# Constant matmuls at four seams of a two-block layer kernel

## The reference

```
# first layer
hn     = rmsnorm(x) * norm_g                       # seam "x" is here
proj   = hn @ w_in                                 # 2048 x 12292
ya, yb, yc = three attentions of 4 heads (forgetting, chunked relpos, stick breaking)
merged = sum_n sigmoid(gates_n) * ((y_n * silu(g_n)) @ w_up_n)
x1     = x + merged @ w_out                        # seam "merged" is before this product
# second layer: GLA and mLSTM heads, both directions, context of 256 tokens first
ctx scan inputs = (rmsnorm(ctx) * (1+sc) + sh) @ w_in_2
lat scan inputs = (rmsnorm(x1)  * (1+sc) + sh) @ w_in_2
y      = concat(norm(gla) * silu(..), sigmoid(..) * norm(mlstm))
x2     = x1 + gt1 * (y @ w_out_2)                  # seam "y" is before this product
h2     = rmsnorm(x2) * (1+sc2) + sh2               # seam "x2" is here
out    = rmsnorm(x2 + gt2 * ((silu(conv3x3(h2 @ w_up_gate)) * (h2 @ w_up_val)) @ w_down))
```

## Time and profile before

| | |
|---|---|
| time, median of 3 runs | 2298.99 us (2298.82 to 2306.23) |
| time of the profiled execution | 2298.3 us |
| its span, first to last instruction | 2296.6 us |
| PE busy | 2207.8 us (96%) |
| DVE busy | 1547.5 us (67%) |
| ACT busy | 1052.8 us (46%) |
| mean granted TensorE clock | 0.990 |

### The profile page before, as it was taken

How to read it: one execution, slowest core, us unless ns; L and a number is a source line. 1 busy time by engine, 2 the same in 40 slices (tenths; PEclk the granted TensorE clock), 3 DMA queues, 4 the chain that set the end, 5 groups by cost and what they waited for, 6 DMA issues and landing times.

```text
span 2296.6 us, 29599 instructions
## 1 busy us (share of the span) xinstructions
PE 2207.8 (96%) x10304; PEld 1771.3 (77%) x10304; DVE 1547.5 (67%) x2220; ACT 1052.8 (46%) x1317; POOL 50.7 (2%) x99
## 2 busy tenths in 40 slices
PE   7999999999999999999999998989999999999997
PEld 6777778778887777876887776668888888888886
DVE  5455667767676878675665778557777777775554
ACT  4443435544443535446333444345455555554443
POOL 0000000000001000000000000100000000000000
PEclk9999999999999999999999999999999999999999
DMA  7877778878776979774443323555555556566664
GB/s 272 286 248 255 269 239 275 292 241 277 252 270 225 323 267 347 256 275 129 129 128 120 91 84 92 179 184 171 178 190 184 190 176 200 168 199 226 195 192 130
DMA packets 279625, 482.41 MB, mean 210 GB/s; under 512 B 21687, under 2 KB 112905, under 8 KB 277601
## 3 DMA queue, kind: packets, MB, share of 16 engines
q1 hardware_dynamic: 274464, 464.87, 61.4%
q0 software_dynamic: 5056, 16.15, 2.1%
HBM read 474.49 MB, written 6.46 MB: 209 GB/s over the span
## 4 chain that ended last, share of the span: by engine, by line
PE 81%; DVE 8%; ACT 4%; issue 4%; DMA 2%; SPq 0%; ACTq 0%; DVEq 0%; POOL 0%; POOLq 0%
PE gemm_ps L1647 71%; DVE w_lo L971 2%; ACT w_hi L587 2%; DVE msum L1123 1%; PE ps L1676 1%; PE ps L2022 1%; DVE tmpT L1003 1%; PE ps L2074 1%; PE ps L2160 1%; PE ps L2081 1%; DMA w_raw<-in_w_out_dram 1%; DVE sc L1492 1%; DMA mraw<-in_w_mod_dram 0%; PE ps L1718 0%; DMA w_raw<-in_w_in_dram 0%
## 5 line engine op out<-in xcount | busy, mean ns | idle before, releaser
L971 DVE TENSOR_TENSOR w_lo<-w_raw,w_hi 128x1024 fp32r<-128x1024 f32 (+1 forms) x688 | 827.6, 1215 | 488.0 <-ACT w_hi L587 481.5
L1647 PE MATMUL gemm_ps<-w_hi,a_hi 128*128 128x512 f32 (+1 forms) x2304 | 935.1, 406 | 29.7 <-DVE a_lo L1010 14.5
L587 ACT ACTIVATE w_hi<-w_raw 128x1024 fp32r<-128x1024 f32 (+1 forms) x688 | 710.9, 1049 | 456.0 <-PE gemm_ps L1647 351.4
L1647 PE MATMUL gemm_ps<-w_hi,a_lo 128*128 128x512 f32 (+1 forms) x2304 | 900.4, 391 | 0.0
L1647 PE MATMUL gemm_ps<-w_lo,a_hi 128*128 128x512 f32 (+1 forms) x2304 | 898.7, 390 | 0.0
L1647 PEld LDWEIGHTS gemm_ps<-w_hi,a_hi 128*128 128x128 f32 x2304 | 435.7, 189 | 151.7 <-issue 35.6
L1647 PEld LDWEIGHTS gemm_ps<-w_lo,a_hi 128*128 128x128 f32 x2304 | 436.2, 189 | 91.2 <-issue 8.4
L1647 PEld LDWEIGHTS gemm_ps<-w_hi,a_lo 128*128 128x128 f32 x2304 | 435.0, 189 | 92.6
L1552 DVE SCALAR_TENSOR_TENSOR acc<-gp,cw,acc 128x256 f32<-128x256 f32 x344 | 151.5, 481 | 13.8 <-DVE acc L1552 1.4
L1123 DVE SCALAR_TENSOR_TENSOR msum<-mraw,cs,msum 128x1024 f32<-128x1024 f32 x120 | 153.2, 1277 | 0.9 <-DMA mraw<-in_w_mod_dram 0.2
L1647 PE MATMUL gemm_ps<-w_hi,ft_hi 128*128 128x512 f32 x344 | 135.0, 392 | 2.2 <-DVE w_lo L971 2.2
(11 more groups left out here) (375 smaller groups left out, 1532.3 us busy)
## 6 DMA issues: line engine op xcount, KB each, us to landing
w_raw<-in_w_in_dram SPq DMA_DIRECT2D x336, 512.0 KB, 4.5
mraw<-in_w_mod_dram SPq DMA_DIRECT2D x192, 512.0 KB, 6.1
w_raw<-in_w_up_dram SPq DMA_DIRECT2D x336, 256.0 KB, 3.2
w_raw<-in_w_down_dram SPq DMA_DIRECT2D x84, 512.0 KB, 4.2
w_raw<-in_w_out_dram SPq DMA_DIRECT2D x64, 512.0 KB, 4.7
w_raw<-in_w_up_dram SPq DMA_DIRECT2D x24, 512.0 KB, 5.4
x_d<-xres POOLq DMA_DIRECT2D x2, 2048.0 KB, 7.9
x_sb<-in_x_dram SPq DMA_DIRECT2D x2, 1024.0 KB, 5.9
```

Of the source, the lines that this page charges most:

```text
L587: act.activation(w_hi[:, slot, :, 0:n], raw[:, slot, :, 0:n], ACT.Copy).then_inc(hi_done, 1)
L971: dve.tensor_tensor(w_lo[:, slot, :, 0:n], raw[:, slot, :, 0:n], w_hi[:, slot, :, 0:n].bitcast(F32), ALU.subtract).then_inc(lo_done, 1)
L1647: mm = pe.matmul(gemm_ps[:, bank, rt, 0:n], x[:, chunk0 + k, tok], w[:, slot, kk, 0:n], start=(k == 0 and part == 0), stop=(k == chunks - ...
```

## The change

A helper `keep_busy(bank, n)` multiplies the identity with the first 512 columns of `cst`, n times, into the first half of the bank that the next block will begin anew. Nothing reads these values. The calls are in float32. There are 32 of them: at seam x four before the wait for `diag_set` and five behind the first two turns; at merged five before and three behind; at y four behind; at x2 eight before and three behind. Since the helper reads columns beyond the identity, a wait for `const_in` is added ahead of the first four.

```
+            def keep_busy(bank, n):
+                for _ in range(n):
+                    pe.matmul(gemm_ps[:, bank, 0], ident, cst[:, 0:NBLK], start=True, stop=True)
+
             def product(u0, slot0, bank, hi, lo, units, chunk0=0, after=None, chunks=None, n=NBLK,
                         halfway=None, turning=None, turned=None,
-                        turning_next=None):
+                        turning_next=None, busy=(0, 0)):
                 if turning:
                     turned = turning[0]
+                    keep_busy(bank, busy[0])
                     turn(*turning, 0)
                     turn(*turning, 1)
+                    keep_busy(bank, busy[1])
...
             pe.transpose(pC[:, 0:88], vrows[0:88, :], ident[0:88, 0:88]).then_inc(S("n_vecT"), 1)
+            pe.wait_ge(S("const_in"), 16)
+            keep_busy(0, 4)
             pe.wait_ge(S("diag_set"), 1)
...
-                            turning=("x", x_sb, True, 0) if B == 0 else None)
+                            turning=("x", x_sb, True, 0) if B == 0 else None, busy=(0, 5))
...
                 product(U_OUT + BU * c, 0, c % 2, a_hi, a_lo, BU, turning=("merged", merged, False, 0) if c == 0 else None,
-                        after=after, turning_next=("ctx", ctx_sb, False, 0) if c == DC - 1 else None)
+                        busy=(5, 3), after=after, turning_next=("ctx", ctx_sb, False, 0) if c == DC - 1 else None)
...
-                        halfway=(lambda u: half_step(8 * 12 + u)) if c == 0 else None, turning=("y", y, False, KC // 2) if c == 0 else None)
+                        halfway=(lambda u: half_step(8 * 12 + u)) if c == 0 else None, turning=("y", y, False, KC // 2) if c == 0 else None,
+                        busy=(0, 4))
...
-                        turning=("x2", y, False, 0) if isinstance(b, int) and b == 0 else None,
+                        turning=("x2", y, False, 0) if isinstance(b, int) and b == 0 else None, busy=(8, 3),
```

## The result

The changed kernel takes 2315.89 us (median of 7 runs, 2311.49 to 2316.76) against 2300.26 us of the kernel before on the same chips (7 runs, 2297.75 to 2306.71). The medians differ by 15.6 us. The ratio, which goes by all runs and not by the two medians, is 1.0057, about 13 us, with a 95% interval of 1.0044 to 1.0071: 10 to 16 us slower. Forecast were 15.4 us and a time of 2313.7. Effects of the experiments are given by this ratio too.

What follows compares the result with a forecast made beforehand. TensorE, busy for 96% of the span, was taken to bound the kernel. Seams of 9.2 + 2.1 + 1.05 + 3.0 = 15.4 us, added to 2298.3, gave 2313.7 us; range 2306 to 2321.

Steps and rivals of the forecast that it cites:

- Seam x: First block: turns and calls behind the constants' wait move product start from 19.68 to 30.5, less 1.6 clock: +9.2 us.
- Seam merged: Where TensorE awaits merged: calls start behind L1227, product 5.0 us later, less 2.9 from the clock: +2.1 us.
- upper bound of +4.9: At merged: the cost in us if the clock level falls within the calls and stays low for 5.5 us.
- Seam y: Four calls behind the turns end at 1430.6, product formerly started at 1429.52; no clock to win: +1.05 us.
- Seam x2: Eight calls before the turns, three behind; product starts at 1553.0 instead of 1547.95, less 2.0 clock: +3.0 us.
- room of 3.7 us: At x2, time from L2148's end of issue to the rows being ready, against 6.9 us for eight calls.
- Sum: All four seams: 9.2 + 2.1 + 1.05 + 3.0 = 15.4 us slower, giving 2313.7 us.
- Half price: Rival for all calls: each takes 0.43 us instead of 0.86; +4.2 us in all, 2302.5; chance 0.09.
- The constants don't arrive in time: Rival claimed the opposite at x: constants land before 10.5, whole change +6.5 us, 2304.8; chance 0.05.
- hidden filler: Rival at all seams: calls lie in TensorE's waiting time and the clock comes back; 6.5 us faster, 2291.8; chance 0.03.
- the most the seams could win: Product at full clock gives back 1.6 us at x, 2.9 at merged, 0 at y, 2.0 at x2: 6.5 us.

Runs made afterwards that it cites:

- the two half experiments: Kernel before, changed at seam x only: the constants' wait without calls (one execution, 2304.72 us); nine calls on columns of x without that wait (one execution, 2300.17 us).
- the last run: Changed kernel with all 32 calls, the nine of seam x on columns of x, without the constants' wait: 2306.31 us, ratio 1.0030 to the kernel before.

## Why the prediction was right

- **Seam x.** Predicted a product start at 30.5 and +9.2 us; the trace has 30.46 and +9.6. The constants landed a little earlier (first call at 18.60, not 19.4), the eight rows took 6.2 us and not 5.1. The two errors nearly cancel, and that the start came out to 0.1 us is luck. The 0.4 us that are left lie in the first unit: I gave it 2.73 us at full clock, and behind a call it takes 3.15 (30.46 to 33.61), since its first two matmuls start 0.63 us apart; it is 3.16 at merged and 3.14 at x2. The reasoning that the turns stand behind the new wait, and that five more calls outlast a_lo, is shown by the two half experiments: +2.4 and +0.6 to +1.5 alone, +9.6 together.
- **Seam merged.** Predicted +2.1; +2.5. My sum also counted the 0.35 us of slow transposes behind the first unit, which a seam as measured here leaves out; with them the change costs +2.2. The calls stand behind L1227 as read from the wait's number, and three ahead of it with two behind the turns save 5.0 us against five and three. The upper bound of +4.9 for a level that falls within the calls was near what one execution of the version without the wait had, +4.2. The level held in the profiled execution, but it need not have.
- **Seam y.** Predicted +1.05; 0. This is the step that failed. The product does start late: its first six matmuls are done 5.93 us behind the last one ahead of the seam (1440.94 to 1446.87), against 5.00 before (1426.02 to 1431.02), +0.9. But the turn behind the second unit is at 1453.23, 12.29 us behind that matmul, against 12.28 before. The 1.15 us in which the second unit used to wait for its a_lo are now 0.22. The wait before, and the rows after:

```profile
1435.43 0.50 PE L1647 MATMUL gemm_ps<-w_hi,a_hi 128*128 128x512 f32 x1 [1.15 <-DVE a_lo L1010]
...
1442.05 3.60 PE L1627 MATMUL gemm_ps<-cst 128*128 128x512 f32 x8
1445.08 0.79 PE L1654 MATMUL gemm_ps<-w_hi,a_hi 128*128 128x512 f32 x1
...
1450.36 0.50 PE L1654 MATMUL gemm_ps<-w_hi,a_hi 128*128 128x512 f32 x1 [0.22 <-DVE a_lo L1010]
...
1453.23 0.60 PE L1725 MATMUL ps<-cst,xn 128*128 128x128 f32 x4
```

  The two other traces with four calls at y agree (12.27 and 12.30 us). I had looked only at the first wait of this block, and the next one swallowed the delay. The 1.05 us too many here were partly made up by 0.4 us too few at x, which is luck.
- **Seam x2.** Predicted +3.0; +3.0. The room of 3.7 us against eight calls, and the low level at their start, are both in the trace; with three and two calls the seam is 4.6 us shorter.
- **Sum.** Seams 9.6 + 2.5 + 0 + 3.0 = 15.1 us against 15.4 predicted; the runs give 10 to 16, 13 by the ratio. A sum of single seams, one of which (x) moves by itself from 22.59 to 24.96, isn't as exact as a miss of 0.3 us suggests. The total of the profiled execution, +18.1 us, holds 3 us of drift that no seam explains.
- **The rivals.** Half price is out: 64 rows for 32 calls. The constants don't arrive in time; the last run, which does without their wait, shows what it would have been: 4 to 9 us slower, where I had given 6.5. The mechanism of the hidden filler, with chance 0.03, is right wherever calls stand ahead of the wait and fit: a version made so is 5 to 11 us faster than before, around the 6.5 us that I gave as the most the seams could win. That figure counted only product matmuls at the low level. The turns gain too: 8 rows take 1.94 us at x2 before and 1.04 in the changed kernel.

## What to carry to other kernels

Work that shall keep TensorE warm must stand ahead of the wait that it is to cover, and its length must fit that wait; put behind the semaphore that ends the wait, it is paid for with its own time (4.4 us for five calls at merged), less what the clock gives back. An overrun costs nothing only if a later wait of the same engine swallows it, as 0.9 us at y: follow the chain to the next waits, not only to the first. Check what the filler itself has to wait for: a late operand here turned calls worth 0.6 to 1.5 us into 9.6. Price a filler by its rows at both clock levels, and ask what the clock can give back at most (here 6.5 us) before adding 27 us of it.

## What was not expected of the hardware

- At merged the level fell in all five traces without calls there, each with both waits open, 2.62 us ahead of the turns and about 1.7 behind them. With the second one covered and the first left open it held (8.67 us for the seam), in one execution. In two of the five it fell under the turns, before the second wait, and once it fell within calls behind the first wait (15.34 us). When it falls isn't settled by these runs.
- At seam x the same instructions ran at different levels. The first unit took 2.85 us in the run with calls only at merged (19.74 to 22.59) and 5.29 us in the run with two calls each at merged and y (19.67 to 24.96), both with the old seam x; with the wait for the constants alone it took 2.85 too.
- At x2 one call fewer made the turns punctual and the seam 0.7 us longer, since the level came back later. This is one execution against two.
